# The opening of a two-block kernel: adaLN in units of two k-tiles, and x loaded ahead of the weights

## The reference

```python
shift, scale, gate = jnp.split(jax.nn.silu(c) @ ada_w[l] + ada_b[l], 3, axis=-1)
h = rmsnorm(x, norm_g[l]) * (1.0 + scale[:, None]) + shift[:, None]
kc, vc = (hc @ w_in[l])[..., OFF_K:OFF_POOL]     # keys and values, for both streams
q, k, v, up, uf, g = split_proj(h @ w_in[l])
```

## Time and profile before

| | |
|---|---|
| median of 3 runs | 2306.19 us (2303.28 to 2308.52) |
| the profiled execution, its own time | 2305.2 us |
| its span | 2303.4 us |
| PE busy in the span | 97% |
| PE busy from 0 to 55.4 us, before the first kv matmul | 29.68 of 55.4 us |
| PE busy from 55.4 to 159.3 us, up to the end of the last kv chunk | 95.16 of 103.9 us |
| transfer rate in these two stretches | 354 and 323 GB/s |

### The profile page before, as it was taken

One profiled execution on the slowest core, in us unless ns is written; L12 is line 12 of the kernel. 1 busy time (PEld: TensorE's weight loads), 2 busy tenths in 40 slices (PEclk: granted clock), 3 DMA queues, 4 the chain that ended last, 5 costly groups with the idle time before them and its releaser, 6 DMA issues.

```text
span 2303.4 us, 29995 instructions
## 1 busy us (share of the span) xinstructions
PE 2232.2 (97%) x11739; PEld 1826.5 (79%) x11739; DVE 1415.7 (61%) x2216; ACT 1035.4 (45%) x1587; POOL 269.6 (12%) x326
## 2 busy tenths in 40 slices
PE   5999999999999999999999999999999999999998
PEld 2567777778888767678888887888888888888887
DVE  3354543368788365546777777677755777567764
ACT  2232332341422354445555475555544555355553
POOL 1001000000011122100021343111100110001111
PEclk8999999999999999999999999999999999999999
DMA  9875343346665485635566555666556565566653
GB/s 355 307 288 183 121 146 126 117 150 218 233 196 175 158 282 198 205 96 174 185 215 187 167 157 168 195 190 187 188 194 192 184 193 188 195 190 185 193 192 116
DMA packets 322428, 437.14 MB, mean 190 GB/s; under 512 B 13848, under 2 KB 220112, under 8 KB 321264
## 3 DMA queue, kind: packets, MB, share of 16 engines
q1 hardware_dynamic: 316800, 413.19, 55.6%
q0 software_dynamic: 3392, 16.90, 2.1%
q10 hardware_dynamic: 2096, 5.15, 0.6%
HBM read 428.89 MB, written 6.29 MB: 189 GB/s over the span
## 4 chain that ended last, share of the span: by engine, by line
PE 86%; DVE 5%; ACT 3%; DMA 2%; issue 2%; POOL 1%; SPq 0%; ACTq 0%; POOLq 0%; DVEq 0%
PE ps L1409 24%; PE ps L1412 12%; PE ps L1396 9%; PE ps L1398 9%; PE ps L1397 9%; PE ps L1428 5%; PE ps L1430 5%; PE ps L1429 5%; PE ps L1376 2%; DVE SPL L1894 2%; ACT SPL L1642 1%; PE ps L1485 1%; PE ps L1502 1%; DMA RAW<-in_w_in_dram 1%; DMA RAW<-in_ada_w_dram 1%
## 5 line engine op out<-in xcount | busy, mean ns | idle before, releaser
L1894 DVE TENSOR_TENSOR SPL<-RAW,SPL 128x1024 fp32r<-128x1024 f32 x592 | 750.1, 1269 | 535.0 <-ACT SPL L1642 532.4
L1409 PE MATMUL ps<-HS,SPL 128*128 128x512 f32 x2688 | 850.5, 398 | 6.9 <-DVE SPL L1894 3.6
L1642 ACT ACTIVATE SPL<-RAW 128x1024 fp32r<-128x1024 f32 x592 | 622.7, 1056 | 481.0 <-PE ps L1398 176.4
L1412 PEld LDWEIGHTS ps<-HS,SPL 128*128 128x128 f32 x2688 | 504.9, 188 | 119.3
L1412 PE MATMUL ps<-HS,SPL 128*128 128x256 f32 x2688 | 528.4, 278 | 0.0
L1409 PEld LDWEIGHTS ps<-HS,SPL 128*128 128x128 f32 x2688 | 410.5, 189 | 12.2 <-issue 5.5
L1396 PE MATMUL ps<-SPL,HS 128*128 128x512 f32 x960 | 397.0, 414 | 15.9 <-DVE SPL L1894 6.4
L1398 PE MATMUL ps<-SPL,HS 128*128 128x512 f32 x960 | 377.6, 393 | 0.0
L1397 PE MATMUL ps<-SPL,HS 128*128 128x512 f32 x960 | 377.2, 393 | 0.0
L1396 PEld LDWEIGHTS ps<-SPL,HS 128*128 128x128 f32 x960 | 182.3, 190 | 78.3 <-issue 22.2
L1397 PEld LDWEIGHTS ps<-SPL,HS 128*128 128x128 f32 x960 | 182.6, 190 | 41.4 <-issue 6.0
(11 more groups left out here) (296 smaller groups left out, 1827.8 us busy)
## 6 DMA issues: line engine op xcount, KB each, us to landing
RAW<-in_w_in_dram SPq DMA_DIRECT2D x208, 512.0 KB, 4.8
RAW<-in_ada_w_dram SPq DMA_DIRECT2D x192, 512.0 KB, 4.9
RAW<-in_ffn_w_up_dram SPq DMA_DIRECT2D x192, 512.0 KB, 3.6
RAW<-in_w_out_dram SPq DMA_DIRECT2D x96, 512.0 KB, 4.5
RAW<-in_ffn_w_down_dram SPq DMA_DIRECT2D x96, 512.0 KB, 4.2
x_spill<-XT POOLq DMA_DIRECT2D x2, 2048.0 KB, 14.8
XT<-x_spill POOLq DMA_DIRECT2D x1, 4096.0 KB, 15.1
MM<-in_x_dram ACTq DMA_DIRECT2D x2, 1024.0 KB, 11.6
```

The source lines that it names most:

```text
L1409: mm(PS[g.banks[j]][:, :], wr, hh, start=k == 0, stop=False, skip_group_check=True)
L1412: m = mm(PS[g.banks[j]][:, 256:512], wl, hh[:, 0:256], start=False, stop=k == KT - 1, skip_group_check=True)
L1642: act(SPL[:, (n - 1) % NSPL, 0, :], raw_of(i), ACT.Copy).then_inc(s_hi, 1)
L1894: tt(w[:, 1, :], raw_of(s["i"]), w[:, 0, :].bitcast(F32), ALU.subtract).then_inc(s_lo, 1)
```

## The change

The opening's adaLN comes in eight units of two k-tiles. A unit is a group of 256 scale columns and one of 256 shift columns, each in four chunks of 512 rows by 256 columns (form "half"). Both halves go to one bank, the scale half in columns 0 to 255, the shift half in 256 to 511; the bank is 6 or 7 by turns. A chunk now makes four matmuls of 256 columns in place of two of 512. There is one `ada_out` and one turn for a unit, hence still eight in all. DVE does two sums, two bias additions and one scale factor a unit.

A unit is followed by the h tiles of two k-tiles (4 of them). kv chunk v - 1 stands behind the second chunk of unit v, and the early chunks stand at the end of units 3, 5 and 7. Splits are laid one place ahead (two if the next chunk is fm) in the opening, not three. `x` goes first on SP's queue, ahead of the weights, and `ctx` alone on ACT's. The transposes go by token tile, and all 64 of them stand before the first adaLN chunk.

```diff
-START_AHEAD = 3
+        def places_ahead():
+            if at["pos"] > at["opening"]:
+                return at["ahead"]
+            return 2 if queue[at["pos"] + 1].shape == 4 else 1
...
-            while at["taken"] < min(len(queue), at["pos"] + (START_AHEAD if at["pos"] < 76 else at["ahead"])):
+            while at["taken"] < min(len(queue), at["pos"] + places_ahead()):
...
-                if c.shape == 0:
-                    pop_side((2 if i < 8 or i >= 28 else 4) if c.group.side == 2 and c.kc % 2 == 0 else 0)
+                if c.group.form == "half":
+                    pop_side({0: 18, 2: 1, 3: 1, 4: 2, 6: 1}.get(i, 0) if i < 8 else 8 if c.kc == 1 else 1)
...
+        def ada_pair(v):
+            bank = 6 + v % 2
+            def after():
+                slot = ada_out(bank)
+                while len(hi) < 1:
+                    hi.append(idle)
+                hi.insert(1, lambda: ada_turn(slot, 0, bank, [(16 + 2 * v, 2, 0), (2 * v, 2, 2)]))
+            scales = group("half", "ada", I["ada_w"][0, :, :], D + v * 256, [bank], None)
+            shifts = group("half", "ada", I["ada_w"][0, :, :], v * 256, [bank], after)
+            shifts[0].group.second = 1
+            return scales + shifts
...
-                hi.extend(staged([tile_h(0, k, s, x, h) for k in range(4 * u, 4 * u + 4) for s in range(2)])
+                hi.extend(staged([tile_h(0, k, s, x, h) for k in (2 * v, 2 * v + 1) for s in range(2)])
...
-                return cs[:8] + kv[2 * u - 2:2 * u - 1] + cs[8:12] + kv[2 * u - 1:2 * u] + cs[12:] + early[u - 1:u]
+                return cs[:2] + (kv[v - 1:v] if v else []) + cs[2:] + (early[v // 2 - 1:v // 2] if v % 2 and v > 1 else [])
...
-                main = [c for u in range(4) for c in start(u)] + kv[6:7] + early[3:4] + kv[7:8], q0 + q1 + gp + gf + gates
+                main = [c for v in range(8) for c in start(v)] + early[3:4] + kv[7:8], q0 + q1 + gp + gf + gates
...
+                    if g.form == "half":
...
+                        o = PS[g.banks[0]][:, 256 * g.second:256 * g.second + 256]
+                        for q in range(4):
+                            k = 4 * kc + q
+                            m = mm(o[32 * q:32 * q + 32, :], CW[:, 2 * k:2 * k + 32], raw_of(i)[:, q * 256:(q + 1) * 256],
+                                   start=kc == 0, stop=kc == 3, skip_group_check=True)
...
+            for t in range(2):
+                e.dma_start(MX[:, t, :], I["x"][0, t * 128:(t + 1) * 128, :]).then_inc(s_x[t], 16)
```

More of the change, by code:

```diff
@@ L415, in ada_sums, with ada_out, ada_turn, ada_group @@
             return cs
-        def ada_group(l, g, side=0):
-            def after():
[L419 to L423, removed]
-                    hi.append(idle)
[L425 to L435, removed]
+        def ada_out(bank):
+            slot, last = take()
+            s = put("ada_out", slot=slot, bank=bank, last=[multiplied(), *last])
+            bank_last[bank] = [(s_adaE, s["n"])]
+            return slot
+        def ada_turn(slot, l, bank, parts):
+            s = put("ada_turn", slot=slot, l=l, bank=bank, parts=parts, after=use(bank), out=tick("ada_out_columns"))
+            give(slot, (s_adaT, s["n"]))
+            for j, nb, _ in parts:
+                columns_ready(l, j, nb, s["out"])
+            bank_last[bank] = [(s_ada, s["out"])]
+        def ada_group(l, g):
+            def after():
+                slot = ada_out(6)
+                while len(hi) < 3:
+                    hi.append(idle)
+                hi.insert(3, lambda: ada_turn(slot, l, 7, [(4 * g, 4, 0)]))
+            return group("ada", "ada", I["ada_w"][l, :, :], g * 512, [6], after, side=0)
+        def ada_pair(v):
[9 more added lines that the diff above has]
+            return scales + shifts
         def columns(blocks, is_last):
@@ L842, in f @@
                 def f():
-                    s = put("x_out", l=l, j0=j0, banks=banks, last=[multiplied(), ada_ready[l, 8 + j0 // 4]], half=count.get("half", 0), srcs=range(2))
+                    s = put("x_out", l=l, j0=j0, banks=banks, last=[multiplied(), ada_ready[l, 32 + j0]], half=count.get("half", 0), srcs=range(2))
                     n = tick("res", 2) - 1
@@ L858, in last_out @@
                 banks = FRONT if src == 0 else BACK
-                s = put("x_out", l=0, j0=14, banks=banks, last=[multiplied() if src else (s_part, tick("part")), ada_ready[0, 11]], half=0, srcs=[src])
+                s = put("x_out", l=0, j0=14, banks=banks, last=[multiplied() if src else (s_part, tick("part")), ada_ready[0, 46]], half=0, srcs=[src])
                 n = tick("res", 2) - 1
@@ L1184, in two_block_program @@
         queue.extend(chunks)
+        at["opening"] = max(i for i, c in enumerate(chunks) if c.group.form == "half") + 1
         def first_rstd():
@@ L1196, in two_block_program, with turn_x @@
         count["columns"] = 1
-        hi.extend([lambda: put("square_x")] + [idle] * 6 + [lambda: (columns([0, 1, 3, 4], False), columns([5, 6], True))])
-        def turn_x(j):
+        def turn_x(i):
             def f():
-                s = put("turn_x", j=j, after=use(j % 3))
-                bank_last[j % 3] = [(s_xt, s["n"])]
-            return f
-        turns = [turn_x(j) for j in range(KT)]
-        hi.extend(turns[:9] + [first_rstd] + turns[9:13] + [first_rows] + turns[13:])
+                s = put("turn_x", t=i // 4, j=i % 4, bank=i % 3, after=use(i % 3))
+                bank_last[i % 3] = [(s_xt, s["n"])]
+            return f
+        hi.extend([lambda: put("square_x")] + [turn_x(i) for i in range(16)] + [first_rstd, lambda: (columns([0, 1, 3, 4], False), columns([5, 6], True)), first_rows])
         project0(marks[0])
@@ L1627, in scalar @@
             e.dma_start(ONES[:, :], I["k_ones"]).then_inc(s_const, 16)
[L1628 to L1629 removed]
+            for t in range(2):
+                e.dma_start(MX[:, 2 + t, :], I["ctx"][0, t * 128:(t + 1) * 128, :]).then_inc(s_x[2 + t], 16)
             e.wait_ge(s_memset, 2)
```

84 lines of the change are left out of this document (48 added, 36 removed).

## The result

| | before | after |
|---|---|---|
| median, same chip | 2307.6 us (6 runs, 2303.3 to 2309.8) | 2322.3 us (6 runs, 2321.3 to 2324.1) |
| the profiled execution, its span | 2303.4 us | 2320.8 us |
| first kv matmul | 55.46 us | 39.36 us |
| first q matmul | 160.44 us | 176.43 us |

The changed kernel is slower: the ratio is 1.0065, with a 95% interval of 1.0053 to 1.0077, and 14.7 us lie between the medians. The forecast was 2316.5 us, in a range from 2304 to 2330.

A forecast was written before the change was run, and what follows sets the result against it. Transfers bound the first 55 us, then mostly PE to 159; the opening would end at 169.9 us against 159.3, so 2305.2 + 10.6 = 2315.8, and 2316.5 us for the median, range 2304 to 2330.

The forecast's parts named there:

- rows of 1 KB: Opening's adaLN loads: 1.51 us a chunk against 1.34, 12%; by the skill's rule 4%, everything 0.9 us earlier.
- The chain from turn to kv: Each unit's turn, sums, h tiles and split before its kv chunk: 7.15 us, PE idle for 6.1.
- The first turn at 28.75: Opening's start: nine adaLN chunks, x, ctx and small tables, 9.26 MB, in by 28.3 us, then 0.45.
- The period and the clock: Between kv chunks: 16.3 us, six make 97.8; clock falls cost 1.7 us each, 6.8 up to chunk 6.
- The tail: From kv chunk 6 to the opening's end: 29.4 us, with 1.1 where early chunk 3 waits for h.
- A first kv matmul later than 38 us would say that x or its columns come late: Sign for the opening's start, where the first kv matmul was forecast at 35.9 us.
- The new matmul: Four adaLN matmuls of 256 columns in place of two of 512: 0.46 us a chunk, 1.0 at most.
- Rival (c): Opening's adaLN matmuls bound by their number, up to 1.0 us a chunk: slower still, 2346 us; chance 0.12.
- the estimate of 2327 by the Trainium skill's rule: Opening's adaLN matmuls at about 81 ns each, 0.65 us a chunk, would give 2327 us.
- Rival (a): Transfers set the opening's pace and the chain is hidden: 16.2 us earlier, 2290 us; chance 0.11.
- Rival (b): Chain as forecast but PE's clock doesn't fall in the gaps: 8.5 us less, 2308 us; chance 0.13.

The follow-up runs named there:

- Experiment 2: Changed kernel with splits two places ahead and kv chunk v - 2, not v - 1, placed in unit v: 2305.1 us, ratio 0.9989.
- 1: Changed kernel with the split of a kv chunk always laid two places ahead: 2321.0 us, ratio 1.0059.
- experiments 6: Changed kernel with the 1/rms columns and rows taken behind adaLN chunks 6 and 7, not the second to the fifth: 2320.3 us, ratio 1.0059.
- experiment 10: Changed kernel with kv one unit later, splits three places ahead, and the 1/rms columns behind adaLN chunks 6 and 7: 2306.5 us, ratio 0.9997.
- experiment 3: Changed kernel with 12 extra unused matmuls of 256 columns in each of the five PE gaps: 2316.1 us, ratio 1.0039.
- experiment 4: Kernel before the change with only x moved to SP's queue, ahead of the weights: 2303.8 us, ratio 0.9981.
- 9: Changed kernel with x back on ACT's queue ahead of ctx, beside the weights: 2327.1 us, ratio 1.0079.
- experiment 8: Kernel before the change with splits one place ahead in the opening, not three: 2332.6 us, ratio 1.0110.
- experiment 7: Changed kernel with kv behind each unit's sixth adaLN chunk, splits two ahead, and 1/rms columns behind adaLN chunks 6 and 7: 2322.1 us, ratio 1.0064.

## Why the prediction came out as it did

The direction and the mechanism were right; the size was low by 4.1 us (10.6 forecast, 14.7 between the medians; 16.0 at the start of q). Two small slips are in the working: 2306.2 and 10.6 give 2316.8 and not 2316.5, and rows of 1 KB at 4% in place of 12% would save about 1.0 us and not 0.9. By its own steps:

- **The chain from turn to kv, 7.15 us, with 6.1 idle, five times.** 7.16 at the first unit, 6.96 at the second; 5.96 idle, then 5.76. The rows of the kernel before held to 0.2 us. Experiment 2 against 1 shows that this chain is the cause, since only the distance that it has on PE was changed.
- **The first turn at 28.75: the step that was mis-sized.** It came at 32.20, 3.4 us late. I had counted x, ctx, nine chunks and the small tables, 9.26 MB, as if the ninth landed when that many bytes had. The bytes came as forecast: 9.3 MB were in at 28.3 us (285 GB/s up to 10 us, 354 in the next 10, 351 behind). But experiments 6 and 10 have the ninth chunk only at 30.8 and 30.7, when 10.1 MB had come in. By the queues' bytes up to 31 us the small tables are 0.50 MB of it and not 0.35, and the rest, 0.7 to 0.8 MB, belongs to chunks behind the ninth, which were under way too. The other 1 us is PE's (the turn is at 31.26 in experiment 10): the 1/rms rows, which I had ready by 24 us, are made from 27.13 to 29.03, adaLN chunks are held behind them, and those eight matmuls and a chunk run at the lower clock (1.97 and 1.08 us). "A first kv matmul later than 38 us would say that x or its columns come late" was therefore half wrong; chiefly the weights did.
- **The period and the clock.** From kv chunk 0 to kv chunk 6 I had 97.8 + 6.8 = 104.6 us; it took 105.3 (39.36 to 144.70). In experiment 3, with the clock held, the same stretch took 97.6 us (38.20 to 135.77): the 97.8 were right, and what the clock adds to them is 7.8 us and not 6.8. Of the clock I said 1.7 us for each of five spells, 8.5 in all; from the first kv matmul to q, experiment 3 saves 9.4 (1.5 to 2.7 us a gap), and 6.2 in the median.
- **The tail, 29.4 us.** It took 30.7, up to 175.4: the wait inside the last early chunk was 2.5 us and not 1.1. The three splits in a row (DVE, 161.84 to 165.25) stand ahead of the last two h2, as I had said, and took longer than I had allowed.
- **The new matmul, 0.46 us a chunk.** 0.467. Rival (c) is refuted, and with it the estimate of 2327 by the Trainium skill's rule (TensorE: Matmul & The Clock Gate, Back-to-back issue gap): the eight records of a chunk take 58 ns each here, and not the 81 that it gives for 128 columns.
- **Rows of 1 KB, 1.51 us a chunk.** They landed 1.50 us apart at full transfer, against 1.36 for rows of 2 KB in experiment 4 (47.48, 48.84 and 50.19 us), 11% more. The 4% that the Trainium skill's rule would give (DMA: Bandwidth & Descriptors, Why small descriptors are slow) is not what this case shows. Past the start the rate wasn't on the path of the changed kernel, but it bounds experiment 2.
- **Rival (a), transfers set the pace.** Not in the changed kernel (286 GB/s), but it becomes true once kv stands a unit later (experiment 2), and then it gives 2305, not 2290: the first kv matmul is at 47.8, as a kv chunk later in the queue also lands later, and PE still waits for three splits.
- **Rival (b), the clock holds.** It fell in all five gaps. With the clock held by experiment 3 the kernel takes 2316, not 2308, since the first turn and the tail of the sum were low too (3.4 us in its trace); the other part of the 8 us is open.

So the 14.7 us are the sum of parts with both signs: x first is worth about 3 us (4 and 9), kv directly behind its unit costs about 16 (2 against 1), the place of the split 1 or nothing (1), and the rest, half as long units read in rows of 1 KB and nine chunks for a first turn, comes out about level once its order is right (2, which has x first too, is 2.6 us ahead of the kernel before). What no run parts is how much of that last level is the row size and how much the ring; and what the medians and the traces of experiments 3 and 4 differ by (4.4 and 2.6 us) stays open.

## What to carry to other kernels

A smaller unit brings its first result sooner, but the time from a unit's last input to its first use need not shrink with it (here 7 us over three engines, for the four h tiles that a kv chunk needs), and where nothing covers it, it is paid once a unit: find for each unit the independent work that stands in that gap, and count it at the time that it really takes on the engine, not at the rate at which its data land. Where engines take their steps in a fixed order, the place of a helper step (here the split, best at three chunks ahead of the three places tried in the kernel before) can be wrong on both sides: too late and it stands behind a step that waits for the consumer, too early and it waits for its data, or for a free buffer, with everything behind it. Before an early start is counted as a gain, ask what ends last; here a kv chunk 16 us sooner ended 16 us later.

## What the runs showed of the hardware that I had not expected

- With several transfers in flight, the ninth chunk was whole only at 30.8 us, when 0.7 to 0.8 MB of chunks behind it in the queue had come in too (experiments 6 and 10, by the bytes of the queues up to 31 us).
- Moving 2 MB from one queue to another ahead of the weights, with the same bytes in all, made the kernel before 3.8 us faster (4).
- One and the same gap was passed at either clock. In experiment 8 PE is idle for 2.95 us ahead of three early chunks. Behind the first (78.38) the matmuls take 0.40 us throughout; behind the second (112.98) the first few do, and from 114.55 on they take 0.63; behind the third (148.12) nearly all up to 151.4 take 0.63. So a price for the clock read at one gap, as in the prediction, is an average at best.
- The clock can fall after the gap is over: in experiment 7 PE is idle for 4.04 us, its matmuls take 0.40 us at first (58.17), and from 59.50 on they take 0.63.
- With identical work behind the first q matmul, that stretch took from 2141.1 to 2147.2 us over the traces.
